# Three transposes moved in a two-block transformer kernel: the dilated sum later in the branch products, the state-space output spread over four gate pieces, and the first tables loaded in the third chunk

## What is computed

```
branches = jnp.stack([o_a, o_b, o_c], axis=2)
proj = jnp.einsum('bsrc,rcd->bsrd', branches, w_branch)
gates = jax.nn.sigmoid(gpre.reshape(b, s, 3, D_MODEL) + gate_bias)
merged = jnp.einsum('bsrd,bsrd->bsd', gates, proj)
return merged @ w_out
```

```
alpha = jax.nn.softmax(jnp.stack(lses), axis=0)
c = jnp.einsum('gbhs,gbhsd->bhsd', alpha, jnp.stack(outs))
```

## Time and profile before

| | us |
|---|---|
| median of 3 runs | 2875.05 |
| lowest and highest | 2873.32 and 2876.47 |
| the profiled execution, its own time | 2873.89 |
| its span | 2872.1 |
| PE busy | 2833.8 |
| DVE busy | 1818.3 |
| ACT busy | 1484.9 |
| POOL busy | 231.8 |

### The profile page before, as it was taken

The page is one execution under the profiler, slowest core; times in us unless marked ns, Lnnn a source line. Parts: engine busy times, 40 slices in busy tenths (PEclk is TensorE's granted clock), DMA queues, the critical chain, the costliest instruction groups (busy, mean ns, idle before and its releaser), DMA issues.

```text
span 2872.1 us, 44744 instructions
## 1 busy us (share of the span) xinstructions
PE 2833.8 (99%) x18188; PEld 2515.0 (88%) x18188; DVE 1818.3 (63%) x2699; ACT 1484.9 (52%) x2304; POOL 231.8 (8%) x187
## 2 busy tenths in 40 slices
PE   9999999999999999999999999999999999999998
PEld 8989879989989879989888887899799888878997
DVE  5655665646655676645568778665554587786654
ACT  5445555445445555444446567544344465675442
POOL 0010001010010011010014100010100131000100
PEclk9999999999999999999999999999999999999999
DMA  6544444555544445555555344555555454445553
GB/s 237 188 167 155 147 153 176 182 181 191 195 162 143 149 152 200 192 190 192 191 180 179 140 154 148 207 199 180 186 195 191 166 199 140 162 148 181 204 200 118
DMA packets 74779, 504.09 MB, mean 176 GB/s; under 512 B 8752, under 2 KB 10448, under 8 KB 18768
## 3 DMA queue, kind: packets, MB, share of 16 engines
q1 hardware_dynamic: 74576, 501.24, 49.0%
HBM read 500.12 MB, written 1.08 MB: 175 GB/s over the span
## 4 chain that ended last, share of the span: by engine, by line
PE 82%; DVE 10%; ACT 5%; POOL 2%; issue 1%; DMA 0%; SPq 0%; DVEq 0%; ACTq 0%; POOLq 0%
PE ps L1491 40%; PE ps L1509 37%; PE ps L1530 2%; DVE wlo L1963 2%; POOL wlo L2420 1%; DVE conv L2258 1%; DVE pr L2360 1%; ACT whi L1695 1%; PE ps L1625 1%; ACT pr L1924 1%; DVE sm L2361 1%; DVE pr L2357 1%; ACT pr L1930 1%; ACT pr L1922 1%; PE ps L1623 1%
## 5 line engine op out<-in xcount | busy, mean ns | idle before, releaser
L1695 ACT ACTIVATE whi<-raw 128x1024 fp32r<-128x1024 f32 (+3 forms) x938 | 976.8, 1043 | 876.0 <-PE ps L1491 444.9
L1963 DVE TENSOR_TENSOR wlo<-raw,whi 128x1024 fp32r<-128x1024 f32 (+2 forms) x894 | 1075.7, 1216 | 302.8 <-ACT whi L1695 301.9
L1509 PE MATMUL ps<-xT_hi,whi 128*128 128x256 f32 x3296 | 927.0, 281 | 1.3 <-DVE v_mla L2185 1.0
L1509 PE MATMUL ps<-xT_lo,whi 128*128 128x256 f32 x3296 | 920.4, 279 | 0.0
L1509 PE MATMUL ps<-xT_hi,wlo 128*128 128x256 f32 x3296 | 919.9, 279 | 0.0
L1509 PEld LDWEIGHTS ps<-xT_hi,whi 128*128 128x128 f32 x3296 | 619.5, 188 | 8.6 <-issue 6.9
L1509 PEld LDWEIGHTS ps<-xT_lo,whi 128*128 128x128 f32 x3296 | 619.7, 188 | 0.5
L1509 PEld LDWEIGHTS ps<-xT_hi,wlo 128*128 128x128 f32 x3296 | 619.4, 188 | 0.0
L1491 PE MATMUL ps<-whi,xT_hi 128*128 128x512 f32 (+2 forms) x1152 | 368.5, 401 | 6.2 <-DVE xT_lo L1986 3.3
L1491 PE MATMUL ps<-wlo,xT_hi 128*128 128x512 f32 (+2 forms) x1152 | 355.5, 389 | 0.1
L1491 PE MATMUL ps<-whi,xT_lo 128*128 128x512 f32 (+2 forms) x1152 | 355.2, 389 | 0.0
(11 more groups left out here) (318 smaller groups left out, 2438.9 us busy)
## 6 DMA issues: line engine op xcount, KB each, us to landing
raw<-in_w SPq DMA_DIRECT2D x436, 1024.0 KB, 4.8
vr<-in_vrows SPq DMA_DIRECT2D x19, 512.0 KB, 5.7
raw<-in_w SPq DMA_DIRECT2D x12, 768.0 KB, 4.2
raw<-in_w SPq DMA_DIRECT2D x10, 896.0 KB, 4.7
sums<-scratch SPq DMA_DIRECT2D x8, 512.0 KB, 4.4
raw<-in_w SPq DMA_DIRECT2D x4, 832.0 KB, 4.5
raw<-in_w SPq DMA_DIRECT2D x4, 576.0 KB, 3.7
x<-in_x SPq DMA_DIRECT2D x2, 512.0 KB, 6.5
```

The lines of the kernel that those rows point to most:

```text
L1509: made = e.matmul(out, ws[:, o:o + 128], xs[:, kt, :], start=kt == 0 and n == 0 and c % 2 == 0, stop=kt == job.nk - 1 and n == 2, skip_gro ...
L1695: e.activation(out, raw, ACT.Copy).then_inc(*mark("hi", i))
L1963: e.tensor_tensor(out, raw, hi.bitcast(F32), sub).then_inc(*mark("lo", i))
```

## The change

In the first block `third` (the dilated sum's transposes, its copy and its subtraction) runs after the first half of the second branch instead of after the second half of the first branch. In the second block it stays where it was, and only the way in which its place is given is new. The four steps of the ssm's output become a fiber behind `heads_c`: one step after each of the four pieces of gate chunk 4, instead of four steps after chunk 3. The tables of the first block are issued from the list `later`, at the third chunk of the first feed-forward part.

```diff
-                      [m["xn"][:, t, :] for t in (0, 1)], self.xn_free, second, third, 1.0)
+                      [m["xn"][:, t, :] for t in (0, 1)], self.xn_free, second, third, (1, 0), 1.0)
...
-    def branches(self, key, l, order, ots, G, gate, dst, dst_free, second, third, plus):
+    def branches(self, key, l, order, ots, G, gate, dst, dst_free, second, third, behind, plus):
...
                 merge(1, toks[1])
-            ots[i].free = (toks[1],)
-            if i == 0:
-                third()
-                assert second not in self.fibers
+                if n:
+                    ots[i].free = (toks[1],)
+                if (i, n) == behind:
+                    third()
+            assert second not in self.fibers
...
             if c == 3:
                 ob_there = ("tr", oT.name, oT.gen, 6)
-                self.to_T([ob[:, t, :] for t in (0, 1)], fence2[0:2], 8, oT, self.col("ssm_norm_g_2", l, 8))
+                self.fibers.append(self.to_T_steps([ob[:, t, :] for t in (0, 1)], fence2[0:2], 8, oT,
+                                                   self.col("ssm_norm_g_2", l, 8)))
...
-                      (ob_there,), second, third, 0.0)
+                      (ob_there,), second, third, (0, 1), 0.0)
...
-        self.do("tables1")
+        self.later.append(lambda: self.do("tables1"))
```

## The result

The changed kernel takes 2883.67 us (median of 7 runs, 2882.88 to 2884.07), the kernel before 2874.17 us in the runs beside it (7 runs, 2873.32 to 2876.47). The ratio is 1.0032, with a 95% interval of 1.0022 to 1.0041. The profiled execution took 2884.07 us, its span is 2882.3 us, 10.2 us more than before. The forecast of 2887.0 us was 3.3 us too high, and the time lies inside its range of 2878 to 2891.

What follows compares the result with a forecast made beforehand. PE, busy 2833.8 of 2872.1 us, was taken as the bound, so added waits are paid in full. Four steps +11.1, dilated sum -0.7, tables 0, clock +1.6 gave +12.0 us: 2887.0 us, range 2878 to 2891.

Steps and rivals of the forecast that it cites:

- The loop through DVE and ACT: Gate chunk 4's head steps: stick starts 3.87 us earlier, then three loops lengthen by 2.99, 2.65, 3.76; +5.5 us a layer.
- the second rival: Gate chunk 4: the heads' pause leaves two of four steps with no head beside them; 2880.1 us, chance 0.12.
- The list of PE's waits: Gate chunk 4: PE waits some 2 us for the second step's bank, 3 before the third, 3.9 at the values.
- The dilated sum: First block's branch products: POOL's additions start 0.6 us earlier, slowing DVE's low halves less; gain 0.35 us a layer, 0.7 in all.
- my bound: Dilated sum's gain over both layers: from a loss of 0.7 us to 1.2 us if all 0.6 us comes through twice.
- the rule of the Trainium skill named there: DVE and POOL's shared port pair is locked for a whole instruction, the loser blocks; dilated sum's gain then 0.6 us a layer.
- The tables: First block's tables issued at the third chunk: costed at nothing; upper bound 3.9 us if the next load were late.
- The clock: Behind the wait at the values of heads 12 and 13, PE's clock falls once in two layers: +1.6 us.
- The total: Whole kernel: 11.1 - 0.7 + 0 + 1.6 = +12.0 us, prediction 2887.0 us, 0.42% slower, chance 0.70.
- The other side: First rival, gate chunk 4: copies and subtractions find gaps, the block's waits go; 2870.5 us, chance 0.13.

Runs made afterwards that it cites:

- steps_split: Against the kernel before: the ssm's output in four steps, transposes and copies ahead of heads_c, subtractions behind it; 2873.31 us, ratio 0.9998.
- steps_alone: Against the kernel before: only the ssm's output in four steps behind the heads' fiber; 2888.66 us, ratio 1.0047.
- steps_half: Against the kernel before: two of the ssm's four steps at once after chunk 3, two in the fiber behind the heads; 2882.74 us in one run.
- steps_ahead: Against the kernel before: the ssm's output in four steps, their fiber put ahead of the heads' fiber; 2887.96 us, ratio 1.0046.
- sum_alone: Against the kernel before: only the dilated sum's transposes moved after the first half of the second branch; 2872.86 us in one run.
- fiber_and_sum: The changed kernel without its third part: tables loaded at the start as before; 2883.61 us, ratio 1.0033 to the kernel before.
- split_and_sum: Against the kernel before: four steps with copies ahead of heads_c and subtractions behind, plus the dilated sum's new place, tables as before; 2871.30 us, ratio 0.9991.
- tables_alone: Against the kernel before: only the first block's tables issued at the third chunk; 2874.94 us in one run.
- steps_early: Against the kernel before: all four steps of the ssm's output at once, ahead of the first gate chunk and the heads' fiber; 2870.61 us, ratio 0.9988.
- early_and_sum: Against the kernel before: the ssm's whole block ahead of the first gate chunk, plus the dilated sum's new place, tables as before; 2869.10 us, ratio 0.9982.

## Why the prediction was right, and where it was not

- **The loop through DVE and ACT** was right in its steps. The first `stick` was to come 3.87 us earlier: 1755.05, with 0.81 us for how much earlier the stretch began, is 3.86. The loops were to be 7.30, 6.96 and 10.50 us: they are 7.29, 6.96 and 10.41. DVE's idle time was to be 2.5 us three times: it is 2.43. The sum was +5.5 us a layer: B says +5.43. Three steps had a head beside them and the pause fell behind them, so the second rival fell too. That steps_split takes the loss away shows that this is the cause.
- **The list of PE's waits** was not right. I gave about 2, 3 and 3.9 us, 8.9 in all, though the sum allowed 5.5 and the 1.91 us that went, 7.4. Measured are 1.55, 0.30, 2.29 and 1.66 us, 5.80; the missing 1.6 us are slower matmuls between them. I had counted time twice: what PE has waited for a bank, it does not wait again at the values.
- **The dilated sum** was mis-sized: "0.6 x 0.57 = 0.35 us are gained". It is 0.61 us. The even rate was the wrong reading of the rows; the 0.6 us that my bound held, and that the rule of the Trainium skill named there gave, is what came. The even rate failed because the two engines' instructions go by turns. That the subtraction keeps its 0.68 us beside POOL was right (0.69).
- **The tables** cost nothing that can be measured, as said.
- **The clock** is the step that failed: "The new one at the values is some 3.9 us, and no wait behind it would hide the slower matmuls", and with it the +1.6 us. The wait at the values was 1.66 us. The clock fell twice in the second block and cost nothing, since it fell behind an earlier wait and the last one shrank by what it took. In steps_alone it fell behind the last wait in one layer, for 6.8 us, and there the mechanism that I had described cost 2.5 us. The reason given for counting it, the longer idle stretch, is not borne out alone either: behind 2.76 us in steps_half, and behind 3.29 us in steps_ahead, where it had fallen some 19 us before, it stayed at 1.00. Why it falls early in one kernel and late in another with the same waits is open.
- **The total.** 10.86 - 1.23 + 0.42 + 0.15 is 10.2; forecast were 11.1 - 0.7 + 1.6 = 12.0. The 1.6 us of the clock, 0.5 us of the sum and 0.2 us of the loops were too much, and 0.6 us of start and rest were not counted, 1.8 us in all. The other 1.5 us of the 3.3 do not come from the working: the forecast was put on a median of three runs, 1.16 us above the profiled execution, and the median of the changed kernel lies 0.40 us below its profiled one.
- **The other side.** That the copies find gaps fell with steps_ahead. That there was something to be had from moving the block was right, but not by spreading it.

## What to carry to other kernels

When work is spread over the steps of a loop that runs through two engines, look at what stands in front of it on the engine that feeds it and what stands behind it on the engine that waits: here 1.6 us of work in a step made the three loops 2.98, 2.65 and 3.67 us longer, and the same work with another instruction between producer and consumer made the first two 0.52 and 0.12 us longer. If the block can be done where the loop is not running, leave it whole and put it there; here that was the fastest place of those tried. And a fall of the clock is only to be counted where no wait follows that it can come out of.

## What the runs showed of the hardware

- A fall of PE's clock has no fixed price. Behind the branch products of the first block's second layer it came in seven of the twelve kernels and stayed away in five. From the first transpose of the merged rows to the values of heads 10 and 11 of the second block it is 690.60 us in the kernel before, 690.72 in sum_alone, 690.67 in the changed one, 690.62 in fiber_and_sum and 690.64 in split_and_sum, without the fall, and 691.15 to 691.34 in steps_alone, steps_ahead, steps_half, steps_split and tables_alone, with it (in steps_early and early_and_sum the early block lies in this stretch). That is 0.4 to 0.7 us, where I had taken 1.6 us from the granted clock of the window; at the start it was 0.9 us, behind the values 2.5 us, ahead of a wait nothing.
- This fall came in six of the seven kernels in which PE had waited 2.4 us for the merged rows, and in one of the five with the moved sum, in which it had waited 1.8 us. With one trace of each kernel that is a hint and no more; if it holds, the moved sum saves somewhat more than its 0.6 us a layer.
- An addition on POOL and a subtraction on DVE that both read two operands from SBUF went by turns, one whole instruction at a time (sum_alone), and a DVE instruction that reads one of its two from PSUM was not slowed.
- The start scatters by 1.5 us at 409 us between kernels that have the same program up to there or differ only in the tables' place (408.61 to 410.08), of which 0.9 us can be a fall of the clock at 21 us. With one profiled execution of each kernel, the distance A repeats within 0.05 us and B within 0.08 us where the program is the same up to there, wherever in B the clock fell or did not, and absolute times do not.
